# An encoder layer on one core: the loads, the scaling of x and the first TensorE products in another order at the start of the program

## What is computed

```python
h = rmsnorm(x, g_mix[l])
u = h @ w_in[l]
y_mla = mla_attention(u[..., :o1], u[..., o1:o2], u[..., o2:o3], positions, ...)
y_conv = conformer_conv(u[..., o3:], w_dw[l], b_dw[l], g_conv_ln[l], b_conv_ln[l])
x = x + jnp.concatenate([y_mla, y_conv], axis=-1) @ w_out[l]
x = x + memory_cross_attention(rmsnorm(x, g_xattn[l]), rmsnorm(mem, g_mem[l]), ...)
x = x + moe_ffn(rmsnorm(x, g_ffn[l]), w_router[l], b_router[l], ...)
```

## Time and profile before

| | us |
|---|---|
| median of 3 runs (lowest, highest) | 1170.17 (1169.79, 1170.35) |
| the profiled execution's own time | 1170.89 |
| its span | 1168.9 |
| TensorE busy, share of the span | 1126.1, 96% |
| VectorE busy | 352.9, 30% |
| ScalarE busy | 217.1, 19% |
| GpSimd busy | 85.1, 7% |
| HBM read | 436.18 MB, 374 GB/s over the span |

### The profile page before, as it was taken

How to read it: one execution, slowest core, us unless ns; L and a number is a source line. 1 busy time by engine, 2 the same in 40 slices (tenths; PEclk the granted TensorE clock), 3 DMA queues, 4 the chain that set the end, 5 groups by cost and what they waited for, 6 DMA issues and landing times.

```text
span 1168.9 us, 16235 instructions
## 1 busy us (share of the span) xinstructions
PE 1126.1 (96%) x5256; PEld 489.7 (42%) x5257; DVE 352.9 (30%) x896; ACT 217.1 (19%) x419; POOL 85.1 (7%) x206
## 2 busy tenths in 40 slices
PE   7999999999999999999999999999999999999996
PEld 5785477543433333333333333333333333333332
DVE  5897313132232222222223222222222222222223
ACT  4312212221111112111111111111111111111112
POOL 2990000000000000000000000000000000000000
PEclk9999999999999999999999999999999999999999
DMA  9437335579999999999999999999999999999993
GB/s 362 181 153 272 154 149 214 218 302 399 428 428 428 426 428 428 430 428 428 427 430 429 427 427 430 429 427 429 428 430 428 428 428 429 428 428 427 430 429 144
DMA packets 38166, 437.55 MB, mean 374 GB/s; under 512 B 5056, under 2 KB 5184, under 8 KB 12800
## 3 DMA queue, kind: packets, MB, share of 16 engines
q1 hardware_dynamic: 37568, 436.20, 88.7%
q10 hardware_dynamic: 576, 1.05, 0.3%
HBM read 436.18 MB, written 1.05 MB: 374 GB/s over the span
## 4 chain that ended last, share of the span: by engine, by line
PE 78%; DMA 20%; DVE 1%; ACT 1%; issue 0%; SPq 0%; ACTq 0%; DVEq 0%
PE bank L1559 29%; DMA ring<-in_w_up_dram 18%; PE bank L1578 17%; PE bank L1509 5%; PE total L1522 5%; PE bank L1239 2%; PE bank L1451 2%; PE bank L1249 2%; PE bank L1258 2%; PE bank L1516 1%; PE bank L1598 1%; PE bank L1411 1%; PE total L1411 1%; DMA ring<-in_w_out_dram 1%; PE bank L1602 1%; PE bank L1609 1%
## 5 line engine op out<-in xcount | busy, mean ns | idle before, releaser
L1559 PE MATMUL bank<-ring,buf_m 128*64 128x512 f32 x2112 | 463.3, 593 | 21.7 <-DMA ring<-in_w_up_dram 21.7
L1559 PEld LDWEIGHTS bank<-ring,buf_m 128*64 128x64 f32 x2112 | 149.8, 137 | 329.1 <-issue 285.4
L1578 PE MATMUL bank<-ring,buf_m 128*64 128x512 f32 x1056 | 239.5, 595 | 0.0
L1173 DVE COPY buf_f<-bank 128x512 f32<-128x512 f32 x33 | 22.8, 691 | 461.9 <-PE bank L1559 461.9
L1578 PEld LDWEIGHTS bank<-ring,buf_m 128*64 128x64 f32 x1056 | 72.8, 136 | 137.6 <-issue 129.2
L774 ACT ACTIVATE buf_f<-bank 128x512 f32<-128x512 f32 x33 | 19.7, 597 | 373.8 <-PE bank L1559 373.8
L1522 PE MATMUL total<-buf_m,wr_sb 64*128 64x512 f32 x272 | 67.6, 615 | 0.8 <-ACT buf_m L785 0.8
L1509 PE MATMUL bank<-buf_k,buf_v 128*64 128x512 f32 x272 | 65.9, 605 | 0.0
L1179 DVE TENSOR_TENSOR buf_f<-bank,buf_v 128x512 f32<-128x512 f32 x66 | 45.3, 687 | 59.5 <-PE bank L1598 59.5
L548 POOL TENSOR_TENSOR buf_v<-table,buf_v 128x4 f32<-128x4 f32 x33 | 6.6, 199 | 779.0 <-DVE buf_v L1161 778.5
L785 ACT ACTIVATE buf_m<-bank,buf_v 128x512 f32<-128x512 f32 x33 | 22.7, 687 | 211.4 <-PE bank L1578 211.4
(11 more groups left out here) (340 smaller groups left out, 870.3 us busy)
## 6 DMA issues: line engine op xcount, KB each, us to landing
ring<-in_w_up_dram SPq DMA_DIRECT2D x128, 2048.0 KB, 31.9
ring<-in_w_down_dram SPq DMA_DIRECT2D x63, 2048.0 KB, 32.2
ring<-in_w_in_dram SPq DMA_DIRECT2D x4, 1024.0 KB, 17.0
ring<-in_w_xkv_dram SPq DMA_DIRECT2D x2, 2048.0 KB, 27.5
ring<-in_w_xkv_dram SPq DMA_DIRECT2D x1, 4096.0 KB, 12.7
ring<-in_w_out_dram SPq DMA_DIRECT2D x1, 4096.0 KB, 12.9
ring<-in_w_xq_dram SPq DMA_DIRECT2D x2, 2048.0 KB, 21.4
ring<-in_w_xo_dram SPq DMA_DIRECT2D x1, 4096.0 KB, 13.9
```

Of the source, the lines that this page charges most:

```text
L1559: ins = t_.matmul(banks[c][h * 64:(h + 1) * 64, :], xg[:, k, :], w[:, h * FF + c * BANK:h * FF + (c + 1) * BANK], start=k == 0, stop=k == ...
L1578: ins = t_.matmul(banks[2][h * 64:(h + 1) * 64, :], actT[:, f, :], group(slot_of(at))[:, part * D + h * BANK:part * D + (h + 1) * BANK], s ...
```

## The change

- x's columns and the weights of the 416 columns are loaded in five pieces instead of four: blocks 0, 1, 2-3, 4-5 and 6-7 (`FIRST`). The semaphores follow.
- On the SP queue, by_channel goes; w_in pieces 0, 1 and 2 are first, then the positions, x0 and x1, and pieces 3 and 4. What follows stays.
- On the ACT queue by_channel is issued between the first and the second of the five xT pieces. The square root on the scrap value waits for `const_ready` 2 instead of 1.
- On GpSimd the memset of ones moves in front of eps and ident.
- On VectorE all five `gained` steps come ahead of the copy of the positions and the angle steps; none is left between these and `rstd("x")`.
- On TensorE eight products of ones with ones (128x128, into a bank that is not used yet, result unused) come first, behind `const_ready` 1.

```diff
+WARM = 8
+FIRST = [(0, 1), (1, 2), (2, 4), (4, 6), (6, 8)]
@@
             def load_pair(i):
-                sp.dma_start(wu_sb[:, 2 * i:2 * i + 2, :], wu_v[:, 2 * i:2 * i + 2, :]).then_inc(loaded[f"wu{i}"], 16)
+                lo, hi = FIRST[i]
+                sp.dma_start(wu_sb[:, lo:hi, :], wu_v[:, lo:hi, :]).then_inc(loaded[f"wu{i}"], 16)
@@
-            sp.dma_start(channel_vecs[:, :], by_channel).then_inc(loaded["by_channel"], 16)
             load_pair(0)
             load_pair(1)
+            load_pair(2)
             sp.dma_start(pos_i, ...).then_inc(loaded["pos"], 16)
             for t in range(TT):
                 sp.dma_start(xs[:, t, :], x[0, t * P:(t + 1) * P, :]).then_inc(loaded[f"x{t}"], 16)
-            load_pair(2)
             load_pair(3)
+            load_pair(4)
@@
+            done(g.memset(ones[:, :], 1.0))
             done(g.memset(eps[:, :], EPS))
...
-            done(g.memset(ones[:, :], 1.0))
@@
-            for i in range(4):
-                act.dma_start(xT[:, 2 * i:2 * i + 2, :], xt_v[:, 2 * i:2 * i + 2, :]).then_inc(loaded[f"xT{i}"], 16)
-            act.wait_ge(const_ready, 1)
+            for i, (lo, hi) in enumerate(FIRST):
+                act.dma_start(xT[:, lo:hi, :], xt_v[:, lo:hi, :]).then_inc(loaded[f"xT{i}"], 16)
+                if i == 0:
+                    act.dma_start(channel_vecs[:, :], by_channel).then_inc(loaded["by_channel"], 16)
+            act.wait_ge(const_ready, 2)
@@
-            gained(0)
-            gained(1)
+            for i in range(len(FIRST)):
+                gained(i)
             dve.wait_ge(loaded["pos"], 16)
@@
-            gained(2)
-            gained(3)
             rstd("x", 0, D)
             on_diagonal(diag_x, 0)
-            dve.wait_ge(h_ready, 4)
+            dve.wait_ge(h_ready, len(FIRST))
@@
+            pe.wait_ge(const_ready, 1)
+            for i in range(WARM):
+                t_.matmul(banks[7][:, 0:P], ones[:, :], ones[:, :], start=True, stop=True)
             pe.wait_ge(const_ready, 4)
@@
+            piece_of = [i for i, (lo, hi) in enumerate(FIRST) for k in range(lo, hi)]
...
-                pe.wait_ge(h_ready, k // 2 + 1)
-                pe.wait_ge(loaded[f"wu{k // 2}"], 16)
+                pe.wait_ge(h_ready, piece_of[k] + 1)
+                pe.wait_ge(loaded[f"wu{piece_of[k]}"], 16)
```

More of the change, by code:

```diff
@@ L257, in wait_drained @@
             eng.wait_ge(drained[drained_at[job][0]], drained_at[job][1])
-        names = ["x0", "x1", "mem", "memT", "pos", "by_channel", "xT0", "xT1", "xT2", "xT3", "wu0", "wu1", "wu2", "wu3",
+        names = ["x0", "x1", "mem", "memT", "pos", "by_channel", "xT0", "xT1", "xT2", "xT3", "xT4", "wu0", "wu1", "wu2", "wu3", "wu4",
                  "wc0", "wc1", "wc2", "wc3", "uq", "ukv", "wk0", "wk1", "wv", "wout", "wxq0", "wxq1", "wxo", "bdown", "router", "bup", "late"]
@@ L831, in gained @@
                 dve.wait_ge(loaded[f"xT{i}"], 16)
-                v.tensor_tensor(hT[:, 2 * i:2 * i + 2, :], xT[:, 2 * i:2 * i + 2, :], bc(gmix_sb[:, 2 * i:2 * i + 2], T),
-                                ALU.mult).then_inc(h_ready, 1)
+                lo, hi = FIRST[i]
+                v.tensor_tensor(hT[:, lo:hi, :], xT[:, lo:hi, :], bc(gmix_sb[:, lo:hi], T), ALU.mult).then_inc(h_ready, 1)
             def on_diagonal(dst, c):
```

## The result

The changed kernel takes 1173.61 us (median of 20 runs, 1170.74 to 1177.66) where the kernel before took 1170.13 us in its 20 runs beside it. The ratio is 1.0026, 95% interval 1.0019 to 1.0033: slower by about 3 us. (One of the 20 runs of the kernel before took 1694 us; the others took 1168.7 to 1171.7.) Its profiled execution took 1174.35 us, with a span of 1172.5.

A forecast was written before the change was run, and what follows sets the result against it. The expert loop's DMA stream was taken to have fixed length, so only its start, set through rx in the trunk, could move. The 1.0 us gain at rx gave 1170.17 - 1.0 = 1169.2 us, range 1168.2 to 1170.7.

The forecast's parts named there:

- Blocks 4 and 5: TensorE's products for these blocks early in the trunk wait for weights landing at 13.2 us; eight records take 2.9 us.
- The constant products: TensorE's eight opening products take 3.6 us, covered by its idle time before the first real product; no cost or gain.
- ACT's issues and GpSimd's order: At kernel start, two more ACT issues of 0.47 us each and reordered GpSimd memsets are hidden, costing nothing.
- The angle steps on VectorE: VectorE's cast, behind the last xT piece landing at 9.95, starts at 10.6; the steps take 4.03 us, ending at 14.63.
- rival B: Early loads come later because small pieces move slowly: 0.85 us leaves gain 0.2 (1170.0), 1.5 us gives 1170.6; chance 0.14.
- The scale of x: On VectorE, rstd directly follows the angle steps at 14.65; 1.67 us later the diagonal is ready, at 16.32.
- rx: TensorE's job that reads VectorE's diagonal starts at 16.4 instead of 17.41, gaining 1.0 us; the bound moves to VectorE.
- x0 and x1: These SP loads of x keep the bytes ahead of them, so the root for rstd stays ready at 13.55 us.
- Rival A: TensorE falls to half rate while waiting for the fourth weight piece: 1170.2, 1171.5 or 1174.7 us; chance 0.10.
- Passing on: Behind rx, the whole 1.0 us shift goes through the trunk to the end, one to one.

## Why the prediction was wrong, step by step

- **Blocks 4 and 5**: weights expected at 13.2, records from 13.5 on. Right. **The constant products**: 3.6 us expected, 3.78 measured, cover as described. The first real record was to come before 6.0 at full rate; it came at 6.08, and the rate was half until 9.57. That had no price in the sum, and none shows. **ACT's issues and GpSimd's order**: cost nothing, as said.
- **The angle steps on VectorE** is the step that failed. It put the last xT piece at 9.95, because two queues were taken to share by bytes (2 x 87.6 thousand bytes / 391 = 0.45 us). They share by packets: the piece landed at 13.2, 3.2 us later than that. The upper bound that I gave it, 0.6 us more, and the 1.5 us of rival B were both far below that, so the range could not hold it. The trace of before had the evidence: the table of the queues for 4 to 5 us, shown above, which the prediction did not read. What the few late packets of the tail add to the 3.2 us is not explained by the packets' sizes. The steps themselves took 4.04 us, against the 4.03 that were said.
- **The scale of x** took 1.68 us, from 17.85 to 19.53, and **rx** was bound by VectorE's diagonal as predicted, only 3.2 us later than the 16.4 of the sum. With the landing put right, the prediction's own steps give 13.2 + 0.65 + 4.03 + 1.67 + 0.1 = 19.65 (19.58 measured). The run with by_channel back on SP, where the piece lands at 10.0, gives 16.50 and 0.9 us of gain in the median.
- **x0 and x1** were said to stay. x0 came 1.0 us earlier (9.80 against 10.81): it got what ACT's queue lost, and by_channel was no longer ahead of it.
- **Rival B** had the right place (xT late, the angle steps behind it) and the wrong reason and size: small pieces are not slow, and its 1.5 us were half of what came. The rule on batching that it drew on (the Trainium skill, "DMA: Bandwidth & Descriptors", section "Bandwidth") is not what these runs turn on.
- **Rival A** had the right mechanism at another place: TensorE stood still for 3.0 us in front of rx and not of the weights, and the granted clock was 0.50 behind it. It adds 1.8 us to the trunk in the profiled execution, a cost that the sum did not have. The second fall, at 245 us, adds 1.34 us there, and the prediction had no such term at all.
- **The order on VectorE alone** was by the sum the source of the gain. With the loads of before it is worth nothing (1.0002), since TensorE's blocks 0 to 3 end too late for it. Once these begin earlier there is room: with by_channel back on SP, TensorE stands in front of the weights of blocks 4 and 5 until 13.64, and the diagonal is ready at 16.24. In the run with the order undone the gain is another one: the cast is at 8.78 instead of 9.73, and blocks 4 and 5 follow at 13.65 instead of 14.51.
- **Passing on**: the shift of 3.97 us at 25 us is 3.85 us at 160, as said. Behind it the one to one did not hold in this execution: 5.19 us in the loop, by the second fall of the clock, and 3.6 us at the end of the span, by a stretch that was slow in the profiled execution of the kernel before.

## What to carry to other kernels

When two DMA queues are both busy, ask for the packets of each, not only for the bytes: here a load of one short packet for each partition took as many turns as one of 4 KB packets, so put small loads on the queue whose packets are large, and let the loads that are waited for have the larger packets. Don't place a wait for a late piece in front of unrelated work on an in-order engine; here the same loads are 1.5 us faster than before, or 3 us slower, by the place of two steps. A part that is free alone may take away the slack on which another part's freedom rests, so cost the parts of a change together.

## What the runs showed of the hardware

- Two queues that both have work take turns packet by packet and move nearly equal numbers: 75 and 74 in 1 us with 2 KB against 4 KB, 123 and 110 with 2 KB against 2 KB, 51 and 48 with 6 KB against mostly 4 bytes. With 2 KB against mostly 4 bytes the counts part: 109 and 225.
- The landing of a load with the same loads around it differs between executions: x's last piece was in at 13.2 and 13.0 us in two traces of the changed kernel, at 12.5 without the constant products and at 12.2 with more of them.
- How long TensorE's first records stay at half rate varies between executions far more than the constant products do to it. The first real record and the end of half rate were at 7.04 and 9.93 before, 6.80 and 13.05 with the order on VectorE alone, 6.08 and 9.57 in the changed kernel (with the products), 5.97 and 10.05 without them; with the products and the large xT load every record was at full rate from 5.95 on.
- The clock was at 0.50 soon after TensorE had stood still for 3.01, 2.68 and 2.31 us, and TensorE was at full rate after 1.46, 1.38 and 0.91 us. A long stand-still isn't needed, though: the fall at 245 us came behind a wait of 0.85 us, and the same wait in the kernel before was followed by none. Over the 20 runs of the changed kernel the time mostly follows the mean granted clock: the four at 0.998 took 1170.7 to 1171.6 us, the seven at 0.995 or less 1173.5 to 1177.7 (one at 0.999 took 1173.8).
